# Products of constants on TensorE inside the waits of a hybrid decoder step

## The reference

```python
for l in range(DEPTH):
    h = rmsnorm(x, P['ffn1_norm'][l])
    x = x + 0.5 * swiglu_ffn(h, P['ffn1_w_gate'][l], P['ffn1_w_up'][l], P['ffn1_w_down'][l])
    h = rmsnorm(x, P['mix_norm'][l])
    cols = h @ P['w_in'][l]
    ...
    y_a = conv_module(u, P['conv_w'][l], P['conv_b'][l], P['conv_ln_g'][l], P['conv_ln_b'][l])
    ...
    y_b = combine_dilations(parts).reshape(B, T, ATTN_W)
    ...
    y_c, S = rwkv_time_mix(cols_c, prev, S0, ...)
    x = x + jnp.concatenate([y_a, y_b, y_c], axis=-1) @ P['w_out'][l]
    h = rmsnorm(x, P['xattn_norm'][l])
    ...
    x = x + cross_attend(h, mk, mv, P['xattn_w_q'][l], P['xattn_w_o'][l])
    h = rmsnorm(x, P['ffn2_norm'][l])
    x = x + 0.5 * swiglu_ffn(h, P['ffn2_w_gate'][l], P['ffn2_w_up'][l], P['ffn2_w_down'][l])
y = rmsnorm(x, P['final_norm'])
```

## Time and profile before

| | |
|---|---|
| three timed runs | 1671.45, 1671.87 (median), 1672.5 us |
| profiled execution, its own time | 1671.88 us |
| span from first to last instruction | 1670.1 us |
| mean granted TensorE clock | 0.984 |
| TensorE products busy | 1593.0 us (95%) |
| VectorE / ScalarE / GpSimd busy | 64% / 45% / 12% |

### The profile page before, as it was taken

The page is one execution under the profiler, slowest core; times in us unless marked ns, Lnnn a source line. Parts: engine busy times, 40 slices in busy tenths (PEclk is TensorE's granted clock), DMA queues, the critical chain, the costliest instruction groups (busy, mean ns, idle before and its releaser), DMA issues.

```text
span 1670.1 us, 32138 instructions
## 1 busy us (share of the span) xinstructions
PE 1593.0 (95%) x13716; PEld 1507.9 (90%) x13716; DVE 1074.7 (64%) x1659; ACT 753.5 (45%) x1293; POOL 207.1 (12%) x190
## 2 busy tenths in 40 slices
PE   8999999999899989999999999998998998999997
PEld 8999999886689779999999999998767896999997
DVE  6776467878563367775477754779875642777744
ACT  5444348324444344443354433573355443544433
POOL 1000000980010010000010000029501000100000
PEclk9999999998999999999999999999979999999999
DMA  6666744303537665445445667442234477544541
GB/s 241 268 248 249 290 161 135 113 20 90 215 117 291 257 252 177 156 172 168 161 159 209 237 254 275 135 149 72 61 120 177 152 287 301 198 173 154 175 164 41
DMA packets 39965, 303.71 MB, mean 182 GB/s; under 512 B 4816, under 2 KB 4976, under 8 KB 7408
## 3 DMA queue, kind: packets, MB, share of 16 engines
q1 hardware_dynamic: 37488, 288.92, 47.8%
q0 software_dynamic: 2048, 11.17, 2.4%
q10 hardware_dynamic: 288, 1.57, 0.3%
HBM read 291.88 MB, written 36.83 MB: 197 GB/s over the span
## 4 chain that ended last, share of the span: by engine, by line
PE 79%; DVE 11%; ACT 5%; DMA 2%; issue 2%; SPq 0%; DVEq 0%; ACTq 0%
PE bank L676 22%; PE bank L678 22%; PE bank L677 21%; PE bank L860 3%; DVE w_lo L1911 3%; ACT w_hi L1385 1%; DMA slots<-stream 1%; ACT arena L1385 1%; PE bank L1285 1%; PE bank L1270 1%; DVE h_mem L1927 1%; PE bank L1339 1%; PE bank L1158 1%; PE bank L824 1%; PE bank L1322 1%
## 5 line engine op out<-in xcount | busy, mean ns | idle before, releaser
L1911 DVE TENSOR_TENSOR w_lo<-slots,w_hi 128x1024 fp32r<-128x1024 f32 x386 | 484.5, 1258 | 339.5 <-ACT w_hi L1385 338.5
L676 PE MATMUL bank<-h_hi,w_hi 128*128 128x288 f32 x1936 | 578.1, 299 | 18.3 <-DVE w_lo L1911 10.5
L677 PE MATMUL bank<-h_lo,w_hi 128*128 128x288 f32 x1936 | 571.9, 295 | 0.0
L678 PE MATMUL bank<-h_hi,w_lo 128*128 128x288 f32 x1936 | 570.0, 294 | 0.0
L1385 ACT CAST w_hi<-slots 128x1024 fp32r<-128x1024 f32 x390 | 406.4, 1046 | 290.0 <-PE bank L678 261.4
L676 PEld LDWEIGHTS bank<-h_hi,w_hi 128*128 128x128 f32 x1936 | 363.6, 188 | 25.9 <-DVE w_lo L1911 10.2
L678 PEld LDWEIGHTS bank<-h_hi,w_lo 128*128 128x128 f32 x1936 | 365.3, 189 | 0.0
L677 PEld LDWEIGHTS bank<-h_lo,w_hi 128*128 128x128 f32 x1936 | 364.3, 188 | 0.3
L678 PE MATMUL bank<-hid_hi,w_lo 128*128 128x288 f32 x704 | 207.7, 295 | 0.0
L677 PE MATMUL bank<-hid_lo,w_hi 128*128 128x288 f32 x704 | 207.3, 294 | 0.0
L676 PE MATMUL bank<-hid_hi,w_hi 128*128 128x288 f32 x704 | 207.1, 294 | 0.0
(11 more groups left out here) (334 smaller groups left out, 2115.6 us busy)
## 6 DMA issues: line engine op xcount, KB each, us to landing
slots<-stream SPq DMA_DIRECT2D x237, 1024.0 KB, 5.0
out_win3k<-win3k SPq DMA_DIRECT2D x2, 4080.0 KB
out_win3v<-win3v SPq DMA_DIRECT2D x2, 4080.0 KB
h_mem<-stream SPq DMA_DIRECT2D x4, 1024.0 KB, 10.6
out_win2k<-win2k SPq DMA_DIRECT2D x2, 2032.0 KB
out_win2v<-win2v SPq DMA_DIRECT2D x2, 2032.0 KB
con<-consts SPq DMA_DIRECT2D x1, 2340.0 KB, 10.8
arena<-mem_in POOLq DMA_DIRECT2D x2, 1024.0 KB, 5.6
```

What stands on the lines that cost most here:

```text
L676: mm(out, lhs[0], rhs[0], start=start, stop=False)
L677: mm(out, lhs[0], rhs[1], start=False, stop=False)
L678: return mm(out, lhs[1], rhs[0], start=False, stop=stop)
L1911: D(tt(out, src, hi.bitcast(F32), ALU.subtract), name)
```

## The change

A helper `keep_busy(b, n)` is added. It multiplies the block of ones by the identity and ones (256 columns, f32) n times into bank b, overwriting what is there (the next real product in that bank starts its sum anew), and signals nobody. It is called behind the claim of the bank and ahead of the next wait: three products in each of the prompt's two solves at the first level, one product at three places of the sample solve, and two products at two places of the first unit of attention. That makes 13 products per layer, with nothing removed and no wait added.

```diff
+                def keep_busy(b, n):
+
+                    for _ in range(n):
+                        mm(bank[b][:, 0:2 * P], ones, con[:, CON["ident"]:CON["ident"] + 2 * P], start=True, stop=True)
+
                 def level_y(ct, m):
                     claim(4 * ct, (SL, ("y", ct, m)))
+                    if m == 0:
+                        keep_busy(4 * ct, 3)
                     if m < len(LEVELS):
                         pe.wait_ge(vector_done, VL.value(l, ("lo", ct, m) if m else ("diag", ct, 0)))
                     pe.wait_ge(vector_done, VL.value(l, ("x", ct, m - 1) if m else ("x0", ct)))
...
                 TL.done(i, "s_y")
+                keep_busy(1, 1)
                 pe.wait_ge(scalar_done, SL.value(l, "s_y"))
...
                 claim(7, (SL, ("u", 2)))
+                keep_busy(7, 1)
                 pe.wait_ge(scalar_done, SL.value(l, ("r", 2)))
...
                 TL.done(i, ("u", 2))
+                keep_busy(6, 1)
                 pe.wait_ge(scalar_done, SL.value(l, ("u", 2)))
...
                         claim(4 + kt, (SL, ("pT", u, kt)))
+                        if u == 0:
+                            keep_busy(4, 2)
                         pe.wait_ge(vector_done, VL.value(l, ("probs", u)))
...
                     claim(b, (SL, ("attn", u)))
+                    if u == 0:
+                        keep_busy(b, 2)
```

## The result

The changed kernel took 1675.36 us (median of 20 runs, 1673.2 to 1678.71) against 1672.02 us (median of 20) for the kernel before: ratio 1.0019, 95% interval 1.0012 to 1.0025. That is 3 us slower, just inside the 0.2% that I called no change, and outside the range of the forecast, on the other side. Timed again later, the ratio was 1.0021 (1.0011 to 1.0031).

The account below looks back on a forecast made before the run. TensorE's products hold most of the chain that ended last, its clock halved in stretches of the mixing stage. 1671.88 - 1.04 (A) - 5.1 (C) + 2.2 (B) = 1667.9 us, -0.24%; range 1664.0 to 1671.5.

Parts of the forecast that it names:

- A: Prompt's first solves: layer 0 gains 1.04 us if the clock is held, layer 1's 0.7 us lateness costs 0.
- C: First unit of attention: products inside waits remove the clock's fall, gaining 2.55 us per layer, -5.1 for both.
- slower: Rival: added products don't hold the clock, falls in the solves and attention stay; 1676.2 us, chance 0.07.
- B: Sample solve: three products at half clock overrun their waits, costing 1.1 us per layer, +2.2 in the sum.
- The rival with the clock back a step earlier: Sample solve: added products bring full clock back earlier; 1666.0 us in one layer, 1664.1 in both; chance 0.25.
- a new fall: Rival: shifted waits make the clock fall elsewhere, candidate the slab wait after 446.16; 1669.6 to 1671.3 us, chance 0.15.

Follow-up runs that it names:

- after: The changed kernel as in the diff, against the kernel before: 1675.36 us, ratio 1.0019; its profiled execution took 1673.28 us.
- a_and_c: The changed kernel without the sample solve's three products, against the kernel before: ratio 1.0010 (0.9998 to 1.0022).
- c_only: Only the two pairs of products in the first unit of attention added to the kernel before: ratio 0.9997 (0.9985 to 1.0009).
- kv_late: The kernel before with GpSimd issuing the store `out_kv` later, no added products: ratio 0.9990 (0.9981 to 0.9999) to the kernel before.
- after_kv_late: The changed kernel with the store `out_kv` issued later, against the kernel before: ratio 1.0001 (0.9986 to 1.0016).
- after_again: The changed kernel, unchanged, timed again against the kernel before on one chip: ratio 1.0021 (1.0011 to 1.0031).
- c_kv_late: Only the first attention unit's products, with `out_kv` issued later, against the kernel before: ratio 0.9986 (0.9975 to 0.9997).
- c_x_kv: First attention unit's products, `out_kv` later, two products in each of the cross attention's last two slab waits, against the kernel before: 0.9976 (0.9964 to 0.9988).
- ac_kv_late: Products of the prompt's solves and first attention unit, without the sample solve's, `out_kv` later, against the kernel before: 1.0005 (0.9992 to 1.0017).
- after_x_kv: The changed kernel with `out_kv` later and two products in each of the cross attention's last two slab waits, against the kernel before: 0.9994 (0.9981 to 1.0007).
- before: The kernel before, without the change: 1672.02 us (median of 20); its profiled execution took 1671.88 us.

## Why the prediction was wrong

**What bounds, and the price of the fall in one place: right.** A gained 0.99 us in layer 0 (49.81 to 48.82; forecast 1.04) and cost 0.06 in layer 1 (48.75 to 48.81 over the same stage; forecast 0). C gained 2.70 and 2.67 us (30.24 to 27.54, 30.21 to 27.54; forecast 2.55). The clock held behind every product of A and C: the mechanism of the rival "slower" did not happen, and that its 1676.2 lies near the measured 1675.36 is chance. In 26 layers of profiles with C's products there is no fall in the units of attention behind them.

**B: the step that failed first.** I took a product at half clock as 0.93 us; the step behind it starts 1.15 us after it (386.34 to 387.49), so its three waits make 0.69, 0.49 and 0.51, 1.69 us of lateness in layer 0 instead of 1.22. The other profiles bear that out. From the end of s_y to the start of the convolution's sums (386.41 to 396.79 in after) TensorE takes 8.66 us in the nine kernels without B's products, at half clock and without a stop, and 10.38 in those with them: 1.72 more. Where the first product still meets a full clock it is 9.85 to 10.17. In the four profiles of the changed kernel B's products cost 3.1 to 3.4 us in both layers together, for the 2.2 in the sum. I also kept all else there as it was. The rival with the clock back a step earlier did not happen: in layer 0 the low stretch was 13.7 us in each of three profiles of the kernel before and 17.1 in each of four of the changed one. But this does not show that the products lengthen it: a_and_c, without B's, has 17.1 too, and so have c_only and kv_late, with neither A's nor B's; after_kv_late, with both, has 13.7. In layer 1 it was 13.7, 17.1 and 13.7 before, and 17.1 and three times 13.7 in the changed kernel. And TensorE stopped 2 us in s_y.

**A: a term that was not in the sum.** The stop stands in s_y because of A's instructions. In nine profiles with A and `out_kv` at its old place it was 0.86 to 3.07 us, mean 1.94; in five without A the stop 12 MATMULs later, in s_xinc, was 0 to 1.07, mean 0.35. That is 1.6 us, more than A's gain. The earlier trace rows show no such stop, and I left out a stop of 0.54 us put down to issue that stands just ahead of them in L1008. The diff adds 12 MATMULs here; I counted their time, not their place in the stream of instructions.

**The falls: a single execution taken for the program.** This is the largest miss. The sum took each fall of the earlier trace rows as certain, and each removed one as gained. I wrote that "where in time the waits come has a part in it" and still gave a new fall only 0.15. The mean granted clock of every timed execution tells the size: at levels of 1.00 and 0.50, twice the missing share of the clock times the span is the time at half clock. In the runs of after_again it is 55.4 us for the kernel before (mean of 21) and 49.0 for the changed one (mean of 11; the clock is on record to 0.001, which is 1.7 us either way in one execution). The forecast took 20.5 us away (three stretches of 6.83); 6.4 went. In the profiles the rest came back in the sample solve, in the cross attention, at 1265 and 1319, and in layer 1 ahead of C.

**The balance.** A straight line of time over half-clock time through these 21 and through these 11 executions gives 1671.6 and 1676.2 us at an equal 50 us of half clock: the change costs 4.6 us (95%: 3.7 to 5.5, from drawing the runs anew). The two terms above, 3.1 to 3.4 us of products in the sample solve and 1.6 us of the stop, make 4.7 to 5.0. The same lines through the runs with one place alone give 2.5 us for A (1.5 to 3.4), 2.3 for B (0.8 to 4.2) and 0.5 for C (-0.5 to 1.4): what the change costs lies in A and B. Some 0.33 us is paid for each us at half clock by the same lines, so the 6.4 us give 2.1 back. 4.6 - 2.1 = 2.5, and the means differ by 2.6. Against the sum, the falls gave 2.1 us for the 6.1 of A and C, 4.0 too few, and the change's own price is 4.6 for 2.2, 2.4 too many. What c_kv_late and c_x_kv gained is, by these lines, less half clock alone: 47.3 us of half clock for 54.5 and 46.8 for 58.0, and at an equal 50 us they differ from the kernel before by 0.0 and 0.1 us.

**What stays open.** The four profiled executions of the changed kernel, 1671.0 to 1673.3 us, all lie below its median of 1675.4, and 10 of 13 profiles of kernels with C lie below their kernel's median. So the timed executions have more falls than the profiles of these kernels show, and which ones is not known; it may be why C alone is worth 2.6 us a layer in the profiles and 0.5 us (-1.5 to 2.5) in the timed runs. What A costs with `out_kv` moved is not known either: at an equal 50 us of half clock ac_kv_late still takes 2.1 us (1.1 to 2.9) more than the kernel before, and it has no stop in s_y. That `out_kv` delays the instruction block is shown for the stop in s_y; how much of the timed difference of 3 us between the changed kernel and after_kv_late is due to it is not, since after_x_kv did not gain it again.

## What to carry to other kernels

One profile shows one draw of the places where the clock falls: before pricing a fall as gained, profile several executions, and price the change at equal half-clock time apart from the change of that time. Work that only fills waits still adds instructions, and a late block of these costs in a place far from the edit; where TensorE's program is a run of tiny products, try to keep large stores off the DMA engines (worth 0.10% here, 0.01 to 0.19). Fill a wait only where it is longer than what goes in: C's products (0.93 us in waits of 1.20 and 0.99) cost nothing that the profiles show, B's (in waits of 0.40 to 0.61, on a chain of turns between two engines) cost 1.7 us a layer.

## What the runs showed of the hardware

- A store of 864 KB from GpSimd's queue kept an instruction block from TensorE for 3.6 us (383.6 against 380.0 with the store moved), and 1.67 to 2.59 us of it were idle time in each of four profiles. It is named only as issue.
- TensorE's instructions come in packets of 16 KB, one for some 256 of them (109 packets for 27,922 instructions in before). In twelve profiles of seven kernels the late block begins at the same instruction, behind 3,491 MATMULs, and TensorE goes on 2.3 to 2.7 us after its packet starts.
- Behind an added product of two passes at half clock the next small step starts 1.15 us after it; doubled from full clock, 3.72 us for 16 passes, it would be 0.93.
- A stage of many engines repeats within 0.15 us between executions and chips where the clock does the same in it (A's stage 48.81 to 48.84 us in eight kernels); a slab transfer does not: the same wait was 1.2 to 3.1 us.
